# Opening and closing the expert stage of a two-layer decoder in another order: four gate/up products ahead of the gather, sums opened with x

## The reference, cut to what matters

```
h = rms_norm(x, ln_ffn_g)
# top-1 of 4 groups, then top-2 of its 8 experts: 2 of 32 experts a token
x = x + sum_e (silu(h @ w_gate[e]) * (h @ w_up[e]) * comb[:, e]) @ w_down[e]
h = rms_norm(x, ln_ple_g)
x = x + sigmoid(h @ w_ple_gate) * (p @ w_ple)
```

## Time and profile before

| | |
|---|---|
| median of 3 runs | 1102.52 us (1100.24 to 1103.07) |
| the profiled execution, own time | 1100.03 us |
| its span, first to last instruction | 1098.2 us |
| TensorE busy | 1037.3 us, 94% |
| VectorE / ScalarE / GpSimd busy | 619.8 / 383.0 / 117.8 us |
| moved by DMA | 300.68 MB, mean 274 GB/s |
| mean granted TensorE clock | 0.995 |

### The profile page before, as it was taken

One profiled execution on the slowest core, in us unless ns is written; L12 is line 12 of the kernel. 1 busy time (PEld: TensorE's weight loads), 2 busy tenths in 40 slices (PEclk: granted clock), 3 DMA queues, 4 the chain that ended last, 5 costly groups with the idle time before them and its releaser, 6 DMA issues. The chain is left out here.

```text
span 1098.2 us, 19810 instructions
## 1 busy us (share of the span) xinstructions
PE 1037.3 (94%) x7908; PEld 825.4 (75%) x7908; DVE 619.8 (56%) x1255; ACT 383.0 (35%) x704; POOL 117.8 (11%) x127
## 2 busy tenths in 40 slices
PE   5999999999999999887989999999999999988886
PEld 4989999999865555444889999999996555544456
DVE  6588999776621221111877899997646122111156
ACT  4356443354421111101653554435443211111143
POOL 0112321120100000000002132120100000000000
PEclk9999999999999999999999999999999999999998
DMA  7559985665689999999454697665648899999962
GB/s 208 140 161 272 322 235 148 174 182 165 234 309 418 417 416 418 416 416 365 138 153 136 196 333 233 192 190 151 189 159 342 328 418 416 417 417 416 417 206 89
DMA packets 202872, 300.68 MB, mean 274 GB/s; under 512 B 13872, under 2 KB 166416, under 8 KB 186384
## 3 DMA queue, kind: packets, MB, share of 16 engines
q1 hardware_dynamic: 202480, 298.76, 76.9%
q10 hardware_dynamic: 288, 0.52, 0.1%
HBM read 298.21 MB, written 1.05 MB: 273 GB/s over the span
## 5 line engine op out<-in xcount | busy, mean ns | idle before, releaser
L786 PE MATMUL ps<-h_pair,wsplit 128*128 128x256 f32 x2880 | 365.4, 286 | 8.4 <-DVE h_pair L2157 4.0
L786 PEld LDWEIGHTS ps<-h_pair,wsplit 128*128 128x128 f32 x2880 | 353.0, 192 | 13.0 <-issue 7.5
L1518 ACT ACTIVATE wsplit<-ring 128x1024 fp32r<-128x1024 f32 x148 | 154.5, 1056 | 179.4 <-PE ps L786 125.9
L2148 DVE TENSOR_TENSOR wsplit<-ring,wsplit 128x1024 fp32r<-128x1024 f32 x148 | 180.2, 1219 | 27.9 <-ACT wsplit L1518 24.6
L2700 DVE TENSOR_TENSOR prow<-prow,ps 128x128 f32<-128x128 f32 x64 | 18.4, 288 | 289.3 <-ACT prow L1805 289.2
L1518 ACT ACTIVATE work<-ps 128x128 f32<-128x128 f32 (+6 forms) x140 | 51.4, 376 | 212.3 <-PE ps L789 187.6
L786 PE MATMUL ps<-gu_ring,hT 128*64 128x256 f32 x896 | 108.3, 385 | 12.8 <-DMA gu_ring<-in_w_exp_up_dram 12.0
L786 PEld LDWEIGHTS ps<-gu_ring,hT 128*64 128x64 f32 x896 | 63.3, 137 | 55.8 <-DMA gu_ring<-in_w_exp_up_dram 15.1
L2289 DVE SCALAR_TENSOR_TENSOR work<-work,convT 128x256 f32<-128x256 f32 x240 | 104.9, 505 | 0.0
L786 PE MATMUL ps<-down_ring,work 128*64 128x512 f32 x320 | 75.8, 594 | 0.9 <-ACT work L1518 0.9
L1805 ACT ACTIVATE prow<-ps 128x128 f32<-128x128 f32 x64 | 17.7, 277 | 129.2 <-PE ps L786 129.2
(11 more groups left out here) (233 smaller groups left out, 1229.3 us busy)
## 6 DMA issues: line engine op xcount, KB each, us to landing
ring<-in_w_in_dram SPq DMA_DIRECT2D x104, 512.0 KB, 4.5
down_ring<-in_w_exp_down_dram SPq DMA_DIRECT2D x40, 1024.0 KB, 21.1
gu_ring<-in_w_exp_gate_dram SPq DMA_DIRECT2D x28, 1024.0 KB, 16.7
gu_ring<-in_w_exp_up_dram SPq DMA_DIRECT2D x28, 1024.0 KB, 18.8
lent_down<-in_w_exp_down_dram SPq DMA_DIRECT2D x24, 1024.0 KB, 21.0
gu_last<-in_w_exp_gate_dram SPq DMA_DIRECT2D x12, 1024.0 KB, 15.4
gu_last<-in_w_exp_up_dram SPq DMA_DIRECT2D x12, 1024.0 KB, 17.4
ring<-in_w_exp_gate_dram SPq DMA_DIRECT2D x12, 1024.0 KB, 16.7
```

The lines of the kernel that those rows point to most:

```text
L786: return nc.tensor.matmul(o, lhsT, rhs, start=first, stop=last)
L1518: return nc.scalar.activation(o, i, ACT.Copy)
L2148: TT(tile_split[:, m, 1, :, :], tile_of(name, m), tile_split[:, m, 0, :, :].bitcast(F32), ALU.subtract).then_inc(tile_low, 1)
```

## The change

In the paired branch it does six things.

1. TensorE runs `gate_up` of places 0 to 3 (EARLY = 4) one after another, into banks 0, 1, 5 and 6 (`hidden_bank`), then two transposes, then the whole gather, which now has two banks (4 and 7) in place of four, then down 0 and 1, and gate_up 4.
2. Banks 4 to 7 are opened by a float32 product of the unit matrix with x, in place of a product of zeros; the sums thus come out with x in them. GpSimd no longer makes the zeros.
3. SP's order follows: gate/up of places 5 to 8 stand together ahead of down 5.
4. Places 11, 21 and 31 come in halves: the first half of gate and of up, then the second; `gate_up(k, 1)` waits for `half_loaded`. The first half of pg0 is issued ahead of down 30 and 31.
5. The last pair's high and low parts are made in two column halves each, and the last combine waits for each by itself. pg0's first tile is split before them.
6. `high_pair` and `low_pair` read the sums in PSUM; `take_sum` (a copy) replaces `add_sum` and comes later. The filler products stay in the last layer only.

Three semaphores are merged into one (`choice_step`), and the statistics of the norm "ple" move from bank 3 to 5.

```
--- before.py
+++ after.py
         def gather_bank(c):
-            return ps[:, 4 + c % 4, :]
+            return ps[:, 4 + 3 * (c % 2), :]
+        def hidden_bank(k):
+            return (0, 1, 5, 6)[k] if k < EARLY else k % 2
...
+                if place >= ERING and place % BODY == BY_HALVES:
+                    for half, loaded in enumerate((gu_loaded[s], half_loaded)):
+                        c = slice(half * SLOT // 2, (half + 1) * SLOT // 2)
+                        for i, w in enumerate((gate_flat, up_flat)):
+                            fill(gate_up_slot(s)[:, i, c], w[expert_at(place, it) + l * NE].rearrange("(q c) f -> q (c f)", q=P)[:, c], loaded)
+                    return
...
-                load_gate_up(l, ERING)
-                with sp.Fori(0, (NE - ERING) // BODY) as it:
-                    for place in range(ERING, ERING + BODY):
+                for place in range(ERING, ERING + EARLY):
+                    load_gate_up(l, place)
+                load_down(l, ERING)
+                load_down(l, ERING + 1)
+                load_gate_up(l, ERING + EARLY)
+                for place in range(ERING + 2, ERING + EARLY):
+                    load_down(l, place)
+                with sp.Fori(0, (NE - ERING - EARLY) // BODY) as it:
+                    for place in range(ERING + EARLY, ERING + EARLY + BODY):
                         load_gate_up(l, place + 1, it=it)
                         load_down(l, place, it=it)
...
-                for c in CHUNKS[CI["wo3"] + 1:]:
+                load_chunk(l, "pg0", (0,))
+                load_down(l, NE - 2)
+                load_down(l, NE - 1)
+                load_chunk(l, "pg0", (1,))
+                for c in CHUNKS[CI["pg0"] + 1:]:
                     load_chunk(l, c)
...
-                def clear_sums(b):
-                    zeros = work_r[:, 4096:4096 + 2 * S]
-                    mm(ps[:, b, :], zeros[:, 0:P], zeros, True, False)
+                def open_sum(b):
+                    m = b - 4
+                    mm(two(ps[:, b, :]), ident, xT[:, 2 * m:2 * m + 2, :], True, False)
...
+                    for k in range(EARLY):
+                        gate_up(k, 0)
+                        gate_up(k, 1)
+                        if k == 1:
+                            weigh_rows()
+                    turn_hidden(0)
+                    turn_hidden(1)
+                    gather(range(DC))
+                    down(0)
+                    down(1)
+                    gate_up(4, 0)
+                    gate_up(4, 1)
+                    spread_places()
+                    pe.wait_ge(xs_read, 2 * DC)
+                    clear((4, 7))
+                    turn_hidden(2)
+                    turn_hidden(3)
+                    down(2)
+                    pe.wait_ge(hhT_ready, 4)
+                    clear((5, 6))
+                    combine(0, False)
+                    down(3)
...
                 with pe.If(most_pe <= windows):
                     paired_experts()
-                    keep_busy(3, 2)
                     if l + 1 == DEPTH:
+                        keep_busy(3, 2)
                         gate_of_last()
...
                 def high_pair(i):
-                    act.wait_ge(x_added, 4 * l + i + 1)
+                    act.wait_ge(summed, 1 * l + 1)
                     for c in (2 * i, 2 * i + 1):
-                        last = nc.scalar.activation(p_high[:, c, :], xT[:, c, :], ACT.Copy, scale=vcol("ple", c))
+                        last = nc.scalar.activation(p_high[:, c, :], two(ps[:, 4 + i, :])[:, c % 2, :], ACT.Copy, scale=vcol("ple", c))
...
-                    low_tile(l, "pg0", 0)
-                    dve.wait_ge(summed, 1 * l + 1)
-                    add_sum(0)
-                    add_sum(1)
+                    for m in tiles:
+                        low_tile(l, "pg0", m)
                     low_pair(0)
-                    add_sum(2)
                     low_pair(1)
-                    add_sum(3)
+                    take_sum(0)
                     low_pair(2)
+                    take_sum(1)
                     low_pair(3)
+                    take_sum(2)
+                    take_sum(3)
                     low_tile(l, "pg0", 1)
```

More of the change, by code:

```diff
@@ L42 @@
 KP = 2
+EARLY = 4
 BODY = 2 * ERING
@@ L45 @@
 PEEL = NE % BODY
+BY_HALVES = (NE - 1) % BODY
 EPS = 1e-6
@@ L609, in source, with load_chunk @@
                 return [cols(w_ple_gate[l], 256 * m, 256)]
-            def load_chunk(l, name):
+            def load_chunk(l, name, halves=(0, 1)):
                 n = CI[name]
@@ L623, in load_chunk @@
                 for half, src in enumerate(parts):
+                    if half not in halves:
+                        at += src.shape[1] * src.shape[2]
+                        continue
                     if before in SI:
@@ L1374, in gate_up @@
                                 at = c * FH + j * P
-                                last = mm(two(ps[j * WIN:(j + 1) * WIN, k % 2, 0:2 * P]), xw[:, k // 2 % 2, c, :],
+                                last = mm(two(ps[j * WIN:(j + 1) * WIN, hidden_bank(k), 0:2 * P]), xw[:, k // 2 % 2, c, :],
                                           gate_up_slot(s)[:, :, at:at + P], c == 0, c == DC - 1)
@@ L1401, in combine @@
                         pe.wait_ge(window_sel_ready, k // 2 + 1)
-                        pe.wait_ge(y_low, k // 2 + 1)
+                        if not final:
+                            pe.wait_ge(y_low, k // 2 + 1)
                         for part in range(2):
                             for i in range(4):
+                                if final and i % 2 == 0:
+                                    pe.wait_ge((y_high, y_low)[part], k // 2 + 1 + i // 2)
                                 for j in range(2):
@@ L1410, in combine, with clear @@
                             last.then_inc(summed, 1)
-                    def step(k):
-                        one_before = k >= 1 and k <= NE
+                    def clear(banks):
+                        for b in banks:
+                            open_sum(b)
+                    for k in range(EARLY):
[4 more added lines that the diff above has]
+                    turn_hidden(0)
@@ L1426, in step @@
-                        if one_before:
-                            turn_hidden(k - 1)
-                        if k >= 3 and k % 2:
-                            combine(k - 3, k > NE)
-                        if k < NE and k != 1:
-                            gate_up(k, 1)
-                        if k in (1, 2):
-                            gather(range(4 * k - 4, 4 * k))
-                        if one_before:
+                        if k <= NE:
+                            turn_hidden(k - 1)
@@ L1435, in step @@
+                        if k % 2:
+                            combine(k - 3, k > NE)
+                        if k < NE:
+                            gate_up(k, 1)
+                        if k <= NE:
                             down(k - 1)
-                    for k in range(NE + 2):
-                        step(k)
                 wait_evacuated(pe, l, "rank")
@@ L1447, in open_gate @@
                     free_bank("pg0")
-                    outs = two(bank("pg0"))[:, 0, :], ps[:, 4, 0:S]
+                    outs = two(bank("pg0"))[:, 0, :], ps[:, 3, 0:S]
                     first = DC // 2 * ROWS.index("ple")
@@ L1811, in take_hidden @@
                     def take_hidden(k):
                         act.wait_ge(hh_tr, k + 1)
-                        copy(hhT[:, k % 2, :], ps[:, k % 2, 2 * P:3 * P]).then_inc(hhT_ready, 1)
-                    def step(k):
-                        one_before = k >= 1 and k <= NE
-                        if one_before:
+                        if 2 <= k < EARLY:
+                            act.wait_ge(down_ready, NE * (l + 1) + k - 1)
+                        copy(hhT[:, k % 2, :], ps[:, hidden_bank(k), 2 * P:3 * P]).then_inc(hhT_ready, 1)
@@ new lines, in paired_experts @@
+                    for k in range(EARLY):
+                        sigmoid(k)
+                    take_hidden(0)
+                    take_hidden(1)
+                    take_gathered(range(DC))
+                    take_high(0)
+                    act.wait_ge(spread_psum, 2)
+                    copy(place, two(ps[:, 3, :])).then_inc(places_spread, 1)
+                    take_hidden(2)
+                    take_hidden(3)
+                    for k in range(EARLY + 1, NE + 2):
+                        if k <= NE:
@@ L1818, in step @@
                             sigmoid(k - 1)
-                        if k == 2:
-                            act.wait_ge(spread_psum, 2)
-                            copy(place, two(ps[:, 3, :])).then_inc(places_spread, 1)
-                        if k >= 3 and k % 2:
+                        if k > NE:
+                            high_tile(l, "pg0", 0)
+                        if k % 2:
                             take_high(k - 3)
```

(6 more changed lines are left out.)

134 lines of the change are left out of this document (74 added, 60 removed).

## The result

| | before | after |
|---|---|---|
| median (20 runs each, same chip) | 1101.38 us | 1104.14 us |
| ratio, 95% interval | | 1.0023 (1.0016 to 1.0031) |
| profiled execution, own time (span) | 1100.03 (1098.2) us | 1106.53 (1104.8) us |
| TensorE / VectorE / ScalarE busy | 1037.3 / 619.8 / 383.0 us | 1042.2 / 619.9 / 382.7 us |

The change costs 2.5 us by the ratio: less than a measurement of this kernel tells from no change by the bound set ahead, yet with 20 runs of each it is there. The two stages of 226 us that were rebuilt end up where they were.

The account below looks back on a forecast made before the run. TensorE was taken to bound the DMA stream until about 330 us, DMA from then on. Per layer, 1.1 us lost in the opening less 1.0 gained at the end, twice, made +0.2: 1102.7 us, range 1096.5 to 1107.5.

Parts of the forecast that it names:

- Unit products, +2.9: Opening: four float32 products replace zeros and add 2.9 us of TensorE work, bounds 0 and +3.5.
- Two-bank gather, +0.5: Opening: two banks leave 0.09 us uncovered for each of six gather chunks, +0.5 us, bounds 0 and +2.
- rival B: Ahead of gate_up 5: slower gather or another hole delays the stream one for one; 1107.7 us at 2.5 us; chance 0.24.
- Gate/up 10 issued 3.9 us later, the stream 1.1 us later: Place 10, each layer: issue at 343.7, begin at 345.3 against 344.2, after 2.5 us of idle stream.
- rival D: Opening: early loads do nothing since the stream's total is fixed; forecast had -1.1 us, not 0; no chance given.
- Six halved places, 0: Three places a layer loaded in halves cost 0 because they queue behind others; the skill's fixed part would give 24 us.
- Down 31 0.8 us earlier by halves and pg0: Stage's end: place 31's halves help, pg0's half ahead holds down 31; gain 0.8 us, bounds 0 and 1.6.
- Last pair, gain 0.9: Stage's end: overlapping column halves cut 2.64 us behind down 31 to 1.7; gain 0.9 us, bounds 0.5 and 1.2.
- The gate's rows from PSUM, loss 0.7: Gate: VectorE finishes tile 1 8.35 us behind the last combine, before 7.64; loss 0.7 us, bounds -0.3 and 1.5.
- Filler gone in layer 0, 0 (covered by tile 1): Layer 0's gate: TensorE ready sooner but ends at the same tile 1, 0 us; without that wait 0 to 1.9 gained.
- Rival C: Layer 0's gate: without filler the granted clock falls to 0.50, products lose 1.5 us; 1104.2 us; chance 0.08.
- Rival A: Opening: unit products cost what zeros do, gate/up 10 begins 2.9 us better each layer; 1096.9 us; chance 0.30.

Follow-up runs that it names:

- e3: The changed kernel with sums opened by zeros and x added ahead of gate_up 20, 22, 24 and 26; 1099.22 us, ratio 0.9976 to the kernel before.
- e5: The changed kernel with places 11, 21 and 31 loaded whole, pg0's first half still ahead of down 30; 1103.24 us, ratio 1.0010 to the kernel before.
- v5: The changed kernel with e3, e5, e6 and e7 together and the filler in layer 0 too; 1095.65 us, ratio 0.9948 to the kernel before.
- v6: v5 with place 31 alone in halves; 1093.53 us, ratio 0.9931 to the kernel before.
- e8: The changed kernel with the last pair's high and low parts each made whole again; 1105.16 us, ratio 1.0022 to the kernel before.
- e1: The changed kernel with the two filler products put back behind layer 0's last combine; 1104.27 us, ratio 1.0015 to the kernel before.
- e6: The changed kernel with TensorE's whole gate of layer 0 written inside both branches, no filler; 1100.86 us, ratio 0.9993 to the kernel before.
- b1: The kernel before with the filler products left out in layer 0 only; 1104.12 us, ratio 1.0016 to the kernel before.
- e7: The changed kernel with VectorE's low part of pg0's second tile moved ahead of the first low rows; 1104.74 us, ratio 1.0025 to the kernel before.
- e4: The changed kernel with gate_up 5 right behind gate_up 4, gate/up 10 issued ahead of downs 7 and 8; 1104.75 us, ratio 1.0016 to the kernel before.
- b2: The kernel before with TensorE's whole gate of layer 0 inside both branches, filler kept; 1101.88 us, ratio 1.0006.

## Why the prediction was right, and where it was not

1102.7 us, within 0.3% of before, was forecast; 1104.14 came, inside the range. What the stage does was right as a mechanism. That the number came so near is partly luck: inside the stage the errors cancel (opening 1.1 us better than forecast, halves 1.3 us worse), and the loss at layer 0's gate was missed altogether.

- **What bounds the stage** (TensorE before place 10, then DMA): right. e3 is the clean test: gate/up 10 goes out 2.5 us earlier, and the stages are 2.5 and 2.9 us shorter.
- **Unit products, +2.9:** 2.6. **Transposes' hole, +0.5:** 0.30. **Two-bank gather, +0.5:** 0.2 (7.98 us for twice 3.91): ScalarE keeps up with two banks, and rival B's price (2.4 us for six chunks) was not paid.
- **Gate/up 10 issued 3.9 us later, the stream 1.1 us later:** the issue came 2.6 us later, and the stream is not later at all: 330 GB/s in the first 52 us in both kernels. The idle stream ahead of place 10 was there (8, 74 and 147 GB/s from 343 to 346 make 2.5 us). So rival D, that the early loads do nothing, is what the opening came to in this kernel.
- **Six halved places, 0:** this failed. By the windows they cost 1.3 us of full rate behind the opening, and by e5 with v5 and v6 1.5 to 1.6 us a layer (1.15 or 0.92 gained with all three places whole, after 0.5 or 0.6 given back at place 31); the 0.2 to 0.3 between the two counts are not explained. I had put this term at nothing because halves queue behind others; they did queue, and were slow while they moved. It is not the fixed part for each transfer of the Trainium skill's page "DMA: Bandwidth & Descriptors" either: that rule gave 24 us, and place 21 shows almost nothing.
- **Down 31 0.8 us earlier by halves and pg0:** it starts 222.80 us behind gate_up 0, 221.96 before, 0.84 later. The slow stream at place 11 (1.3 later) less the halves of place 31 (0.5 by v5 against v6, where I had 0.8) makes 0.8 of it.
- **Last pair, gain 0.9:** 0.67, of which the halves are only 0.12 (e8).
- **The gate's rows from PSUM, loss 0.7:** 0.1. VectorE finishes tile 1 at 532.57, 7.67 us behind the combine, where I had 8.35. It begins 0.92 us behind the combine, where I had 1.05, and its twelve instructions take 5.53 us (525.82 to 531.35), where I had 6.1.
- **Filler gone in layer 0, 0 (covered by tile 1):** this is the step that failed. I took TensorE to be ready as soon as its filler was gone, and did not price the jump between the combine and the gate. Of the 2.76 us that layer 0 lost to the gate's end (238.04 us behind gate_up 0, 235.28 before) 0.17 came in the stage, 1.35 from the late start and 1.24 from the products at the low clock (7.28 us for 6.04, start to start). e1 shows that the missing filler alone does not explain it, e6 that the jump does: there the gate ends 2.5 us earlier.
- **Rival C** (the clock at layer 0's gate) happened, with 1.24 us for the 1.5 forecast. But by itself it cost nothing in e6: the clock fell there too, and tile 1 covered it. Only the late start laid it bare.
- **Rival A** was right in its mechanism and wrong about this kernel: every microsecond less ahead of gate_up 5 is one of the stream (e3), but a float32 product of 512 columns costs 0.9 us (1.72 and 1.91 for two), near the 1.0 taken from the earlier trace rows.

## What to carry to other kernels

When a queue's slots come free by another engine's work, count that engine's work up to the product that frees the slot, and move what can wait (here four products a layer, 5 us in all) to where it idles; moving products against each other only moved the hole. Look for a branch between the last instruction of one stage and the first of the next: a wait whose releaser is "issue", or one that was long over, with an instruction block in the DMA view near its start, was a jump here, and code written into both branches took it away. A gain at the end of a stage is given back by the next thing that is late, so measure to the end of what follows.

## What the runs showed of the hardware that was not expected

- The jump behind the experts cost TensorE 2.6 to 3.0 us from the block's transfer to the first product where one block came, and 3.3 to 4.4 where two came within about a microsecond (e1, b1 above; e7, e8, e4: last block 524.7, 524.7, 524.9, gate 528.00, 528.89, 529.26). From the combine's end to the gate it was 3.98 us in the change, and 4.59 in e7 and 5.32 in e4, which change nothing in TensorE's code near the jump. Where the code lies may decide over this; it was not tried.
- Halved loads (0.5 MB each) ran at 221 to 295 GB/s for three microseconds at place 11, with the DMA engines 91% to 98% busy, and near full rate (408) at place 21. It was not tried what makes the difference.
- The granted clock fell to 0.50 while TensorE stood for 3.44 us behind a filler (e1), and also where the longest of its last waits was 1.12 us (e6: 1.12, 0.70, 0.57, 0.98 us between short bursts). With the filler and no jump (v5, v6, b2) it stayed at 1.00 there.
